# LayerNorm statistics folded onto four partition groups, with the memory projections and the routing arithmetic moved later in the order

## The reference, cut to what matters

```
z = x @ w_in            # q, k, v, conv, memory query, three gates
m = sig(ga)*(A@p_attn) + sig(gc)*(B@p_conv) + sig(gm)*(M@p_mem)
x = LayerNorm(ALPHA*x + m @ w_o)
x = LayerNorm(ALPHA*x + ffn(x))      # layer 0: dense SwiGLU, layer 1: top-2 of 8 experts
```

## Time and profile before

| what | us |
|---|---|
| median of 3 runs | 1580.06 (1577.38 to 1580.95) |
| the profiled execution | 1580.78 |
| its span, first to last instruction | 1579.0 |
| mean granted TensorE clock | 0.993 of full |

### The profile page before, as it was taken

The page is one execution under the profiler, slowest core; times in us unless marked ns, Lnnn a source line. Parts: engine busy times, 40 slices in busy tenths (PEclk is TensorE's granted clock), DMA queues, the critical chain, the costliest instruction groups (busy, mean ns, idle before and its releaser), DMA issues.

```text
span 1579.0 us, 22606 instructions
## 1 busy us (share of the span) xinstructions
PE 1532.7 (97%) x8937; PEld 1353.5 (86%) x8937; DVE 1118.7 (71%) x1023; ACT 922.3 (58%) x958; POOL 151.2 (10%) x190
## 2 busy tenths in 40 slices
PE   7999999999999899999899999999999999999996
PEld 7989899899999799999678888888888888888785
DVE  5546647644444635666688888888888888888987
ACT  4545444433333654444577777777777777767775
POOL 4103003300002103000530000000000000030000
PEclk9999999999999999999999999999999999999998
DMA  9747344874445345433689999999999999999981
GB/s 309 256 125 228 110 132 138 340 240 138 153 141 159 92 141 175 135 107 107 235 296 393 390 384 357 375 381 389 378 349 381 383 388 371 351 390 373 391 316 60
DMA packets 226424, 416.61 MB, mean 264 GB/s; under 512 B 8592, under 2 KB 110368, under 8 KB 224752
## 3 DMA queue, kind: packets, MB, share of 16 engines
q1 hardware_dynamic: 217712, 383.28, 69.1%
q0 software_dynamic: 8608, 31.89, 5.7%
HBM read 393.99 MB, written 23.11 MB: 264 GB/s over the span
## 4 chain that ended last, share of the span: by engine, by line
PE 90%; DVE 4%; DMA 2%; ACT 2%; issue 1%; POOL 1%; SPq 0%; POOLq 0%; ACTq 0%; DVEq 0%
PE ps L1761 12%; PE ps L1762 12%; PE ps L1763 12%; PE ps L2215 10%; PE ps L2217 10%; PE ps L2216 10%; PE ps L2199 5%; PE ps L2201 5%; PE ps L2200 5%; PE ps L2226 1%; DMA mem_v<-in_cache_mem_v_dram 1%; DMA raw<-in_w_mem_k_dram 1%; PE ps L1958 1%; PE ps L1799 1%; PE ps L1829 1%
## 5 line engine op out<-in xcount | busy, mean ns | idle before, releaser
L1230 DVE TENSOR_TENSOR low<-raw,high 128x2048 fp32r<-128x2048 f32 x264 | 603.7, 2291 | 91.1 <-ACT high L900 89.7
L900 ACT ACTIVATE high<-raw 128x2048 fp32r<-128x2048 f32 x264 | 505.9, 1919 | 201.1 <-PE ps L2217 128.0
L1240 DVE TENSOR_TENSOR low<-raw,high 128x2048 fp32r<-128x2048 f32 (+1 forms) x91 | 206.1, 2267 | 204.9 <-ACT high L893 204.8
L1761 PE MATMUL ps<-xh,high 128*128 128x320 f32 x1088 | 342.8, 315 | 7.4 <-DVE xl L1437 6.9
L1762 PE MATMUL ps<-xh,low 128*128 128x320 f32 x1088 | 337.7, 310 | 0.0
L1763 PE MATMUL ps<-xl,high 128*128 128x320 f32 x1088 | 337.5, 310 | 0.0
L2215 PE MATMUL ps<-high,xeh 128*128 128x512 f32 (+1 forms) x768 | 292.4, 381 | 2.8 <-DVE low L1230 1.8
L2217 PE MATMUL ps<-high,xel 128*128 128x512 f32 (+1 forms) x768 | 289.4, 377 | 0.0
L2216 PE MATMUL ps<-low,xeh 128*128 128x512 f32 (+1 forms) x768 | 288.1, 375 | 0.0
L893 ACT ACTIVATE high<-raw 128x2048 fp32r<-128x2048 f32 (+1 forms) x91 | 172.3, 1893 | 161.3 <-PE ps L1763 139.9
L1761 PEld LDWEIGHTS ps<-xh,high 128*128 128x128 f32 x1088 | 206.0, 189 | 16.5 <-issue 14.1
(11 more groups left out here) (362 smaller groups left out, 1620.4 us busy)
## 6 DMA issues: line engine op xcount, KB each, us to landing
raw<-in_exp_w_gate_dram SPq DMA_DIRECT2D x88, 1024.0 KB, 7.4
raw<-in_exp_w_up_dram SPq DMA_DIRECT2D x88, 1024.0 KB, 7.4
raw<-in_exp_w_down_dram SPq DMA_DIRECT2D x88, 1024.0 KB, 6.7
raw<-in_w_in_dram SPq DMA_DIRECT2D x37, 1024.0 KB, 5.3
ybuf<-zeros POOLq DMA_DIRECT2D x12, 1024.0 KB, 17.7
raw<-in_ffn_w_gate_dram SPq DMA_DIRECT2D x11, 1024.0 KB, 5.3
raw<-in_ffn_w_up_dram SPq DMA_DIRECT2D x11, 1024.0 KB, 5.3
raw<-in_w_o_dram SPq DMA_DIRECT2D x8, 1024.0 KB, 5.1
```

What stands on the lines that cost most here:

```text
L900: act.activation(high[(N_DENSE + m) % HI_RING][:, :], raw_moe[s][:, :], ACT.Copy).then_inc(hi_done, 1)
L1230: dve.tensor_tensor(low_moe[s][:, :], raw_moe[s][:, :], high[(N_DENSE + m) % HI_RING][:, :].bitcast(F32), ALU.subtract).then_inc(lo_done, 1)
L1240: dve.tensor_tensor(low[n % RING][:, cols], raw[n % RING][:, cols], high[n % HI_RING][:, cols].bitcast(F32), ALU.subtract).then_inc(lo_don ...
L1761: pe.matmul(out, wh, ah, start=first, stop=False)
```

## The change

1. `STREAM` holds z1 ahead of the four memory units, and each engine does z1 before `memory()`. The transposes of the memory tokens stay behind z0. What stood after unit 0 and after unit 1 (`SLOTS[0]`, `SLOTS[1]`) now both follow `memory()`, behind unit 1.
2. In the LayerNorm POOL sums f = 1 to 5 only. PE takes those sums before the last three k of the last product (in L = 1 before the last product's last stretch), and tiles 6 and 7 and their squares afterwards. `fold_tile` sums over partitions into four groups of 32 partitions, each for 80 of the 320 tokens, so that mean, variance, root and reciprocal are done on 128x80. Four products of one row each spread the reciprocal to all partitions, in PSUM; `normal` reads it there. The full mean for the subtraction is copied by ACT, behind the root. POOL subtracts it from tiles 1 to 4, DVE from 0 and 5 to 7. `KEEP_BUSY` is 3, and stands ahead of the spreading products.
3. The Exp stands behind the last gather copy on ACT; rounds and gates stand in step 6 of the first pair on DVE, places in step 11.

```diff
-STREAM = layer_units(0)[:1] + MEM_UNITS + layer_units(0)[1:] + ffn_units() + layer_units(1)
+STREAM = layer_units(0)[:2] + MEM_UNITS + layer_units(0)[2:] + ffn_units() + layer_units(1)
+GATES_AT, PLACES_AT = 6, 11
+def work_beside(l, i):
+    if l == 0 and i <= 1:
+        return SLOTS[0] + SLOTS[1] if i == 1 else []
+    return SLOTS.get(i, ())
-        POOL_TILES = 4
-        KEEP_BUSY = 7
+        POOL_TILES = (1, 2, 3, 4)
+        OWN_TILES = (0, 5, 6, 7)
+        KEEP_BUSY = 3
+        FOLD = T // 4
+        fold_mean, fold_sq, fold_dev, fold_rstd = (std[:, FOLD * i:FOLD * i + FOLD] for i in range(4))
+        rstd = ps[:, 4:8, 0:FOLD]
...
 # ACT, layer_norm
-                act.activation(std[:, :], std[:, :], ACT.Sqrt, bias=eps[:, 0:1]).then_inc(std_done, 1)
+                act.activation(fold_dev, fold_dev, ACT.Sqrt, bias=eps[:, 0:1]).then_inc(std_done, 1)
+                act.wait_ge(mean_mm, L + 1)
+                act.activation(stats[L % 2][:, MU, :], ps[:, MEAN[L], 0:T], ACT.Copy).then_inc(mean_cp, 1)
 # ACT, DVE and PE, mixer
                     if l == 0 and i == 0:
-                        memory()
+                        for k in range(X_STARTS, len(START)):
+                            start_part(k)
+                        continue
+                    if l == 0 and i == 1:
+                        memory()
 # ACT, ahead of the first pair
-            act.wait_ge(rt_diff, 1)
-            act.activation(pair[:, :, 1:2], pair[:, :, 0:1], ACT.Exp).then_inc(rt_exp, 1)
...
             for c in range(1, 4):
                 gathered(0, c, FIRST_BANK[c], 1.0)
+            act.wait_ge(rt_diff, 1)
+            act.activation(pair[:, :, 1:2], pair[:, :, 0:1], ACT.Exp).then_inc(rt_exp, 1)
             act.activation(row_f[:, 2:3], eps[:, 0:1], ACT.Copy).then_inc(e_silu, 1)
 # DVE, layer_norm
-                dve.tensor_copy(st[:, MU, :], ps[:, MEAN, 0:T]).then_inc(mean_cp, 1)
...
-                dve.reciprocal(std[:, :], std[:, :]).then_inc(rstd_done, 1)
+                dve.wait_ge(fold_mm, L + 1)
+                link(dve.tensor_copy(fold_mean, ps[:, FOLD_MEAN, 0:FOLD]))
+                link(dve.tensor_tensor(fold_sq, fold_mean, fold_mean, ALU.mult))
+                dve.wait_ge(var_mm, L + 1)
+                dve.tensor_tensor(fold_dev, ps[:, FOLD_SQ, 0:FOLD], fold_sq, ALU.subtract).then_inc(var_done, 1)
+                dve.wait_ge(std_done, L + 1)
+                dve.reciprocal(fold_rstd, fold_dev).then_inc(rstd_done, 1)
+                dve.wait_ge(mean_cp, L + 1)
+                centre_late(L, OWN_TILES[0])
+                dve.wait_ge(rstd_mm, L + 1)
...
-                    dve.tensor_tensor(sq[:, f, :], x[:, f, :], std[:, :], ALU.mult).then_inc(normed, 1)
+                    dve.scalar_tensor_tensor(by_fold(sq[:, f, :]), by_fold(x[:, f, :]), float(D), rstd, ALU.mult, ALU.mult
+                                             ).then_inc(normed, 1)
 # DVE, first pair
+                    if first and m == GATES_AT:
+                        rounds_and_gates()
+                    if first and m == PLACES_AT:
+                        places()
 # PE
+            def fold_tile(bank, tile, first, last):
+                for g in range(4):
+                    done = pe.matmul(ps[32 * g:32 * g + 32, bank, 0:FOLD], mean_of[:, 0:32], tile[:, FOLD * g:FOLD * g + FOLD],
+                                     start=first, stop=last)
+                return done
+            def first_sums(L):
+                st = stats[L % 2]
+                pe.wait_ge(summed, 5 * L + 5)
+                mean_tile(MEAN[L], st[:, S1, :], True, False)
+                fold_tile(FOLD_MEAN, st[:, S1, :], True, False)
+                pe.wait_ge(sq_summed, 5 * L + 5)
+                fold_tile(FOLD_SQ, st[:, S2, :], True, False)
             def layer_norm(L):
...
+                mean_tile(MEAN[L], x[:, KD - 2, :], False, False)
+                fold_tile(FOLD_MEAN, x[:, KD - 2, :], False, False)
+                pe.wait_ge(squared, KD * L + KD - 1)
+                fold_tile(FOLD_SQ, st[:, SQ + KD % 2, :], False, False)
                 pe.wait_ge(resid, KD * L + KD)
+                fold_tile(FOLD_MEAN, x[:, KD - 1, :], False, True).then_inc(fold_mm, 1)
                 pe.wait_ge(squared, KD * L + KD)
+                fold_tile(FOLD_SQ, st[:, SQ + (KD - 1) % 2, :], False, True).then_inc(var_mm, 1)
+                mean_tile(MEAN[L], x[:, KD - 1, :], False, True).then_inc(mean_mm, 1)
                 for k in range(KEEP_BUSY):
-                    mean_tile(6, st[:, S1, :], True, True)
+                    mean_tile(BUSY, st[:, S1, :], True, True)
+                pe.wait_ge(rstd_done, L + 1)
+                for g in range(4):
+                    r = slice(32 * g, 32 * g + 1)
+                    last = pe.matmul(rstd[:, g, :], mean_of[r, :], fold_rstd[r, :],
+                                     start=True, stop=True)
+                last.then_inc(rstd_mm, 1)
 # PE, mixer
+                            if u == ("wo", l, 3) and m == 1 and k == KD - 3:
+                                first_sums(2 * l)
 # PE, dense down projection
+                    if f == KD - 1 and k1 == KF:
+                        first_sums(1)
```

More of the change, by code:

```diff
@@ L415, in build_trunk, with by_fold @@
         ps_tr = ps[:, 6:8, :]
-        MEAN, VAR = 4, 5
+        FIRST, BUSY, FOLD_SQ, FOLD_MEAN = 4, 5, 6, 7
+        MEAN = (3, 0, 3)
+        rstd = ps[:, 4:8, 0:FOLD]
+        def by_fold(tile):
+            return tile.rearrange("p (g c) -> p g c", c=FOLD)
         DOWN_BANK = (4, 5, 6, 7, 0, 1, 2, 3)
@@ L774, in sums @@
                 st = stats[L % 2]
-                for f in range(1, KD - 1):
+                for f in range(1, KD - 2):
                     if f == 1:
@@ L789, in centre @@
                 pool.wait_ge(mean_cp, L + 1)
-                for f in range(POOL_TILES):
+                for f in POOL_TILES:
                     pool.tensor_tensor(x[:, f, :], x[:, f, :], stats[L % 2][:, MU, :], ALU.subtract).then_inc(centered, 1)
@@ L918, in memory @@
             def memory():
-                for k in range(X_STARTS, len(START)):
-                    start_part(k)
                 for n, u in enumerate(MEM_UNITS):
@@ L1278, in memory @@
             def memory():
-                for k in range(X_STARTS, len(START)):
-                    start_part(k)
-                lo(AHEAD)
                 for n, u in enumerate(MEM_UNITS):
@@ L1440, in layer_norm @@
                     normal(f)
[L1441 to L1442 removed]
+                    if 2 <= f < 2 + len(OWN_TILES) - 1:
+                        centre_late(L, OWN_TILES[f - 1])
                     if vec is None:
@@ L1474, in mixer @@
                     if l == 0 and i == 0:
+                        for k in range(X_STARTS, len(START)):
+                            start_part(k)
+                    lo(UNIT_OF[u] + AHEAD)
+                    if l == 0 and i == 0:
+                        continue
+                    if l == 0 and i == 1:
                         memory()
-                    else:
-                        lo(UNIT_OF[u] + AHEAD)
                     if u == ("z", l, 6):
@@ L1488, in mixer @@
                         pending = None
-                    for work in SLOTS.get(i, ()):
+                    for work in work_beside(l, i):
                         if work[0] == "turn" or work[0] == "pv" and JOBS[work[1]][0] != "smem":
@@ L1625, in _ @@
             dve.memset(stat[:, 1, 0:1], 0.0).then_inc(e_lo, 1)
-            dve.wait_ge(rt_exp, 1)
-            link(dve.tensor_scalar(pair[:, :, 2:3], pair[:, :, 1:2], 1.0, None, ALU.add))
-            link(dve.reciprocal(pair[:, :, 2:3], pair[:, :, 2:3]))
-            link(dve.tensor_tensor(pair[:, :, 3:4], pair[:, :, 1:2], pair[:, :, 2:3], ALU.mult))
-            dve.tensor_tensor(oh1[:, :, :], oh1[:, :, :], wide(pair[:, :, 2:3]), ALU.mult)
-            link(dve.tensor_tensor(oh2[:, :, :], oh2[:, :, :], wide(pair[:, :, 3:4]), ALU.mult))
-            for k in range(ROUNDS):
-                last = dve.tensor_tensor(gates[:, :, NE * k:NE * k + NE], oh1[:, :, :], oh2[:, :, :], ALU.add)
-            link(last)
             def places():
@@ L1655, in places, with rounds_and_gates @@
                 dve.tensor_copy(place_idx[:, :, :], place_tmp[:, :, :]).then_inc(placed, 1)
-            places()
+            def rounds_and_gates():
+                link(dve.tensor_scalar(cnt[:, 1:2], cnt[:, 0:1], 128.0, float(PAIRS), ALU.is_gt, ALU.mult))
+                link(dve.tensor_scalar(cnt[:, 2:3], cnt[:, 0:1], 256.0, float(PAIRS), ALU.is_gt, ALU.mult))
+                link(dve.tensor_tensor(cnt[:, 3:4], cnt[:, 1:2], cnt[:, 2:3], ALU.add))
+                link(dve.tensor_scalar(cnt[:, 3:4], cnt[:, 3:4], float(PAIRS - 3), None, ALU.add))
+                dve.tensor_copy(total_i[:, :], cnt[:, 3:4]).then_inc(rt_total, 1)
+                dve.wait_ge(rt_exp, 1)
+                link(dve.tensor_scalar(pair[:, :, 2:3], pair[:, :, 1:2], 1.0, None, ALU.add))
```

(19 more changed lines are left out.)

46 lines of the change are left out of this document (15 added, 31 removed).

## The result

The changed kernel takes 1582.90 us (median of 20 runs, 1579.88 to 1584.86), the one before 1580.27 us (20 runs, 1577.18 to 1581.76): a ratio of 1.0017 with a 95% interval of 1.0011 to 1.0023, so 1.7 to 3.6 us slower. That is inside the range, and its 2.6 us are within the 3.2 that the prediction called no change; with 20 runs a side the sign can be told. Its profiled execution took 1583.13 us with a span of 1581.4, 2.4 more than the span of before.

The account below looks back on a forecast made before the run. PE's order of work, 90% of the chain that ended last, was taken as the bound. Terms +2.5 - 3.2 + 1.0 = +0.3 on the profiled 1580.78 us, forecast 1580.5 us, range 1573 to 1586.

Parts of the forecast that it names:

- Part 1: z1 ahead of memory: saves 4.7 us there, costs 5.6 plus 1.6 us waiting for job 0's probs; net +2.5 us.
- X: Time in the new order when the memory units end and job 0's scores start: 54.0 us.
- the exponentials start at X + 6.25 again: ACT's first exponential of job 0, waiting for the memory tiles' DMAs, starts 6.25 us behind the scores, as before.
- Part 2: Folded LayerNorm statistics: gains of 1.55, 1.0 and 0.65 us in the three LayerNorms; net -3.2 us.
- The bound of -8: Best case of the LayerNorm part: 2.0 us gained in each, and no half clock after it in two places.
- the dear folds: Rival: LayerNorm folds cost 68 ns a record, not 23, turning -3.2 us into +0.7, time 1584.5 us; 25%.
- Part 3: Routing moved in the first expert pair: 1.0 + 2.0 + 1.6 - 3.4, net +1.0 us.
- The stall of unit 2: First expert pair: PE's 1.84 us wait for the third `lo` and its 1.6 us half clock go, saving 3.4 us.
- the waits of the two lumps: First expert pair: PE stalls 1.0 us behind step 6's small DVE operations and 2.0 behind step 11's places.
- the second half clock: First expert pair: a half clock behind the stall of step 11, counted only in the upper bound of +2.6 us.
- The probs didn't come in time: Rival: job 0's probs come in time behind z2, making that move -4.7 us and the time about 1573; 12%.
- LayerNorm didn't pay in full: Rival: half clocks after LayerNorm 0 and 1 go with the gap, LayerNorms give -8 us, time 1575.5; 15%.

Follow-up runs that it names:

- e_exp_gap: Changed kernel with memory units back ahead of z1, Exp and the Silu table load moved into idle stretches of ACT: 1577.88 us.
- e_best_no_mem: Changed kernel with memory back ahead of z1, memset ahead of POOL's sums, routing in seven pieces, Exp and Silu table in ACT's idle time: 1571.34 us.
- e_ln_alone: Changed kernel with memory and routing both put back, leaving the folded LayerNorm alone: 1578.49 us.
- e_zeros: Folded LayerNorm alone, with POOL's memset moved ahead of its sums, out of LayerNorm 0: 1576.04 us.
- e_no_mem: Changed kernel with the memory units put back ahead of z1, folds and routing as changed: 1578.55 us.
- e_norm_first: Changed kernel with job 0's normalise moved ahead of the low part on DVE: 1580.27 us.
- e_norm_act: Changed kernel with normalise ahead of the low part and, on ACT, the copy of job 0's transposed probabilities ahead of the high part: 1577.72 us.
- e_busy_after: Folded LayerNorm alone, with four unread mean products behind the spreading products in LayerNorm 0 and 1: 1577.72 us.
- e_best_busy: e_best with four unread mean products behind the spreading products of LayerNorm 0 and 1: 1567.57 us.
- e_best: e_best_no_mem with memory behind z1, normalise ahead of low and the copy of the probabilities ahead of the high part: 1568.24 us, ratio 0.9925 to before.

## Why the prediction was right

Forecast +0.3 on the span, measured +2.4 on it and 2.6 by the medians, with the three parts of the right sign each. That the total came this near is partly luck, for misses of both signs stand in it: by the stretches, parts 1 and 3 cost 2.0 and 1.4 us more than forecast and the LayerNorms and the wait for `mem_v` gave 1.2 more; by the medians, part 1 costs 1.9 more, part 2 gives 1.4 less and part 3 costs 0.9 less.

**Part 1: sign and mechanism right, too small.** Forecast +2.5, measured +4.54 in A and 4.35 by the medians. The memory units end and the scores start at 53.6 (forecast X = 54.0), PE comes to the probs at 62.8 (X + 9.1), and from the first exponential to PE's restart 8.46 us pass (forecast 8.45). The step that failed is "the exponentials start at X + 6.25 again": they start at X + 7.84. The last DMA out of the memory tiles took 6.13 us, by the chain that ended last in the changed kernel:

```profile
55.22 6.13 DMA out_mem_v_prompt_dram<-mv
```

By the lists of DMA issues the four of `mv` landed in 5.8 us instead of 4.6 (medians). Around X the DMA engines were fuller than before. The windows of before and changed (the last columns are PEclk, DMA share, GB/s):

```profile
50.00:52.00 2.00, 2.00 (x18) 1.84 (x18) 0.97 (x2) 0.00 (x0) 0.00 (x0) 1.00 0.40 153
52.00:54.00 2.00, 2.00 (x16) 1.65 (x14) 2.00 (x3) 0.00 (x0) 1.39 (x3) 1.00 0.55 119
```
```profile
52.00:54.00 2.00, 2.00 (x19) 1.84 (x19) 0.97 (x2) 0.00 (x0) 0.00 (x0) 1.00 1.06 374
54.00:56.00 2.00, 2.00 (x19) 1.65 (x16) 2.00 (x3) 0.00 (x0) 1.31 (x3) 1.00 0.89 260
```

That the fuller engines cause the late landing is not shown, and two runs speak against it. In e_exp_gap and e_best_no_mem, with memory ahead of z1, the exponentials also start late, 8.28 and 7.72 us behind the scores; the other six kernels in that order have 6.32 to 6.61, the five with the move 7.72 to 8.12. And in e_exp_gap the DMA share around X is what it is in e_ln_alone, where they start 6.36 us behind the scores at 58.24 (0.60 and 0.40 in the same two windows, scores from 51.91 and 51.88):

```profile
50.00:52.00 2.00, 2.00 (x19) 1.86 (x18) 0.99 (x1) 0.00 (x0) 0.00 (x0) 1.00 0.60 219
52.00:54.00 2.00, 2.00 (x15) 1.62 (x16) 1.98 (x3) 0.00 (x0) 1.00 (x2) 1.00 0.40 63
```
```profile
60.19 0.47 ACT L990 ACTIVATE sc<-ps,small 128x256 f32<-128x256 f32 x1 [11.53 <-DMA out_mem_v_prompt_dram<-mv]
```

What delays the last landing stays open. The rest is the half clock, which lasted from 68 to 74.9 and cost some 2.5 us of work (half of the 5.0 us behind the restart) instead of 1.6.

**Part 2: sign and mechanism right, the size not reached in most runs.** Forecast -3.2. In the changed kernel's own trace LayerNorms 0, 1 and 2 give -0.97, -1.31 and -1.46, -3.7 in all (stretch D's -2.13 holds 0.67 that belongs to a DMA wait on `mem_v`, 0.62 us in the trace of before at layer 1 and absent after). In the six other kernels with the same LayerNorms it is -1.1 to -3.3 by the same count, and by the medians of e_ln_alone -1.8 with the wait on `mem_v` in it. The forecast took the half clock behind LayerNorms 0 and 1 as it was; it lasted 3.4 us behind each in the one trace of before, but 6.8 us behind LayerNorm 0 in all seven and behind LayerNorm 1 in five of them. With 3.4 us behind LayerNorm 1, as before, C gains 1.31 in both traces that have it. How long the half clock lasts in other executions of the kernel before no trace here shows, so the size stays open within these bounds. The bound of -8 for this part does not follow from its own terms: three times 2.0 and two half clocks of 1.6 make 9.2.

The folds cost 26 ns a record (16 from 278.27 to the next product at 278.68), near the 23 taken. The rule of the Trainium skill that spoke for the dear folds (TensorEngine Tiling (Array Packing), Key Properties: a change of mode drains TensorE) shows no price that mattered: mean product, two folds and whatever a change of mode costs took 1.15 us together, from 277.53 to 278.68, of which the mean product by the earlier trace rows is 0.56 and the folds 0.41. `normal` starts 4.4 us behind the last product (4.0 forecast). The contention itself was forecast and is borne out operation by operation: two SBUF operands 1.01 us beside POOL (L1417) against 0.48 alone, a PSUM operand 0.49. That `tensor_scalar` stretches as well, 0.91 beside the centring and 1.65 beside the memset against 0.43 alone, was not in the forecast; it reads one tile of SBUF and a value per partition. The Trainium skill (GPSIMD Engine Reference, Specifications) names instructions in a 2-port performance mode beside those with two SBUF inputs as the ones that contend with POOL; the stretch fits that, but no row here shows the mode in which `tensor_scalar` ran. The 1.2 us of the memset (e_zeros) can't be counted as what the change fell short by: it stood in LayerNorm 0 before as well, where the `tensor_scalar` beside it took 1.48 us against 0.43 alone.

**Part 3: right in each term, wrong in what was left out.** Forecast +1.0, measured +0.11 in E and +2.33 in F (0.1 by the medians, which don't resolve it). The stall of unit 2 went (3.4 us saved), the half clock behind the 2.50 us gap came (0.50 from 795 to 798.5), the waits of the two lumps are 0.55 and 1.79 (forecast 1.0 and 2.0), together 2.3 where 3.0 was said. The step that failed is that the second half clock (839.5 to 842.9) stood among the bounds and not in the sum; it is in all five traces with the lumps and in none of the other eight.

**Rivals.** The probs didn't come in time (PE waited 7.09 us), LayerNorm didn't pay in full (half clocks stood behind LayerNorms 0 and 1), and the folds weren't dear (26 ns where they turn dear from 45).

## What to carry to other kernels

When work is moved into a gap, write down the chain that the gap was covering, with each engine's in-order list, and move the head of that chain as well: here the same move cost 4.4 us with `normalise` and a copy left behind a `high` and a `low`, and was worth 3 us with both in front. Small operations off the critical path go in pieces no longer than the slack of one step, because two lumps of 2.1 and 3.6 us stalled PE where seven pieces did not. Look for operations of another engine that have nothing to do with the critical stretch but stretch its operations by standing beside them, and for table loads that fit an idle stretch: those two edits cost no work and gave 1.2 and 3.2 us in their stretches. Before a gain of 1 or 2 us is read off a pair of traces, read the same stretch in every trace that has the same code there: here that took the gain of the folds from 3.7 us to somewhere between 1.1 and 3.7.

## What the runs showed of the hardware

- The half clock behind a gap lasted about 3.4 us or about 7 us. Behind LayerNorm 0 of the changed kernel it ran from 286.5 to 293.3, behind LayerNorm 1 from 532.3 to 535.7; in e_no_mem behind both some 7 us. It goes with how executions of one program differ: those of e_no_mem run from 1575.77 us at a mean granted clock of 0.993 to 1581.78 at 0.989.
- A gap of about 2 us didn't always bring it: none stands behind the waits of 2.20 and 2.09 us in e_norm_first, one behind 2.15 us in e_norm_act. Gaps of 0.37, 0.88 and 0.86 us behind LayerNorm 1 brought one in e_busy_after, and 0.37, 0.88 and 0.85 us brought none in e_best_busy. No row here tells such cases apart.
- What it costs depends on what PE does in it: nothing measurable for 3.4 us while tiles come one by one (B of e_best and e_best_busy, 336.84 and 337.02; C of the changed kernel and e_best_busy, 149.30 and 149.31), 1.5 us for 7 us (C of e_best, 150.85).
- DVE's `tensor_scalar` of 128x320 took 0.43 us alone, 0.91 beside POOL's centring and 1.65 beside a POOL memset of 1.80 us; an operation with one operand in PSUM took 0.49 beside the centring.
